# Sparse attention on TensorE: four groups of transpositions a head become two

## The chip, the core and the metric

The kernel runs on one core of one Trainium2 chip. The metric is the device time of one execution in microseconds (us), in the median of several. A core has TensorE (PE in the rows; its weight loads are listed apart as PEld), VectorE (DVE), ScalarE (ACT), GpSimd (POOL) and SyncE (SP), each with a queue of its own that it works through in order. They wait for each other through semaphores.

## The reference, cut to what matters

Two transformer blocks over 512 tokens of width 1024. The change lies in the second one's sparse attention, 16 heads of width 128. Each query attends to those 128 earlier keys that score highest with an indexer, and keys and values are shared by all heads:

```python
def dsa_mixer(x, cos_h, sin_h, cos_i, sin_i, w_in, w_out):
    topk = min(TOPK_MAX, L // 4)
    h = x @ w_in
    q = apply_partial_rope(h[..., :o1].reshape(B, L, DSA_HEADS, DSA_HEAD_DIM), cos_h, sin_h)
    k = apply_partial_rope(h[..., o1:o2], cos_h, sin_h)
    v, z = h[..., o2:o3], h[..., o3:o4]
    ...
        _, idx = lax.top_k(score, topk)             # per query, from the indexer
        k_sel, v_sel = gather(k, idx), gather(v, idx)
        logits = jnp.einsum('bthd,btjd->bthj', q_b, k_sel).astype(jnp.float32) * ATTN_SCALE
        logits = jnp.where(valid[:, :, None, :], logits, -jnp.inf)
        probs = jax.nn.softmax(logits, axis=-1).astype(v.dtype)
        return jnp.einsum('bthj,btjd->bthd', probs, v_sel)
    ...
    return (o * jax.nn.silu(z)) @ w_out
```

## The kernel before

Everything is written out by hand: the order in each engine's queue is the order of the code, and each step waits for named steps of the other engines (`S[...]`, one semaphore for each engine and stage; the tables `DSA_PE`, `DSA_ACT`, `DSA_DVE` list the names in that order). Matrix products are made of three products in a rounded format, high x high, high x low and low x high parts (`split_mm`, lines 933 to 935). A weight unit of 128x1024 comes by DMA, GpSimd splits it into its parts, and one unit is 8 blocks of 3 products with 512 columns.

The 512 queries are four tiles of 128. Tile q looks at the first q+1 tiles of keys, so its scores are 128 x 128(q+1), and the keys that the indexer didn't choose are masked out. For head n and tile q the steps are

- `s{q}` (`dsa_score`, TensorE): the scores, into bank 3 (q even) or bank 4 (q odd). Tiles 2 and 3 wait until VectorE has masked tiles 0 and 1 of the same head, since they use the same banks.
- `m{q}` (`dsa_mask`, VectorE, line 3666): scale, add the mask, and the maximum of each row through an accumulator that is read out behind it.
- `e{q}` (`dsa_exp`, ScalarE, line 2624), `r{q}` (reciprocal of the row sum, VectorE, line 3671), `n{q}` (`dsa_normalise`, ScalarE, line 2629).
- `t{q}` (`dsa_turn`, TensorE, line 1827): q+1 transpositions of 128x128 in full fp32, tile 0 into bank 5, tile 1 into bank 6, tile 2 into bank 2, tile 3 into bank 5 again (so it waits for `l0`).
- `h{q}` (ScalarE, line 1925) and `l{q}` (VectorE, line 2685): the high and the low part of the transposed tile, out of the bank.
- `o` (`dsa_values`, TensorE): 12 products with the values, once `l2`, the last of the low parts, is there.

The loop over s in TensorE's part makes one slot a head. It is filled up with the projection of the query of head s+3 (in the last heads with blocks of the output projection), block by block through `fill(first, end)`, so that TensorE has work while VectorE and ScalarE do the softmax of the tiles. In slot s stand score 1 of head s+1, tile 2 of head s, block 0, score 3, block 1, the values of head s, block 2, tile 0 of head s+1, block 3, score 2, blocks 4 and 5, tile 1, blocks 6 and 7, tile 3, and score 0 of head s+2. Slot s = -1, that of head 0, has no tile 2 and no values, and the last gate (24 products) ahead of tile 3.

Of the kernel before, what the change touches and what calls it, by code (L numbers as in the profile page):

```python
# [134 lines left out]
def dsa_unit(name):  # L135
    return U0["dsa"] + DSA_UNITS.index(name)


DSA_PE = [("s1", 1), ("t2", 0), ("s3", 1), ("o", 0), ("t0", 1), ("s2", 1), ("t1", 1), ("t3", 1), ("s0", 2)]
DSA_ACT = [("qf", 1), ("h3", -1), ("h2", -1), ("e0", 0), ("e1", 0), ("n0", 0), ("e3", 0), ("n1", 0), ("h0", 0), ("oh", -1),  # L140
           ("n3", 0), ("qh", 1), ("e2", 0), ("h1", 0), ("n2", 0), ("z", 0)]
DSA_DVE = [("l0", 1), ("ql", 2), ("r2", 1), ("ol", 0), ("l1", 1), ("m0", 2), ("m1", 2), ("l3", 1), ("l2", 1), ("sw", 3), ("r0", 2),
           ("m3", 2), ("ss", 3), ("oz", 1), ("qc", 3), ("r3", 2), ("qa", 3), ("m2", 2)]

# [4 lines left out]
def dsa_late(s):  # L149
    return [n for n in DSA_LATE if n // 2 == DH // 4 + s]  # L150


def dsa_slot(table, s):

    return [f"{op}_{s + off}" for op, off in table
            if 0 <= s + off < DH and not (op in ("oh", "ol") and s + off in DSA_LATE)]
# [55 lines left out]
def build(nc, ins, out):  # L212
    ctx = ExitStack()
    with ctx:
# [332 lines left out]
        def ln_stage(name):  # L547
            e = [f"e{m}" for m in ln_tiles(name)]
            stage(name, 1, ["ph0", "ph1", "s2n"] + [f"sq{m}" for m in range(5)] + ["sq5", e[0], "sq6", "sq7", *e[1:4], "sqrt", *e[4:-2], "hi0", e[-2], "hi1", e[-1],
                                                                            "h0", "h1"]  # L550
                  + [f"{a}{m}" for m in range(2, KD) for a in ("hi", "h")],
                  ["pl0", "pl1", "y0", "y1", "s1", "y2", "s2", "c0", "c1", "y3", "s3", "v1", "c2", "y4", "s4", "v2", "c3", "y5", "s5", "v3", "c4",
                   "y6", "s6", "v4", "c5", "y7", "s7", "v5", "c6", "c7", "v6", "mu", "dl", "dd", "v7", "var", "rs", "a0", "a1", "b0", "b1"]
                  + [x for m in M8 for x in [f"lo{m}"] + ([f"a{m + 2}", f"b{m + 2}"] if m < KD - 2 else [])],
                  ["y0", "y2", "row", "part", "y4", "y6", *projected(e[:2]), "total", *projected(e[2:4]), "squares", "mean", "root", *projected(e[4:])])
# [30 lines left out]
        for n in range(DH + 1):  # L586
            dsa_act += [f"z_{DH - 1}" if x == "z_0" else x for x in dsa_slot(DSA_ACT, n)
                        if x not in ("qf_0", "qf_1") and (x[:2] != "z_" or n == 0)]
            dsa_act += [f"oh_{x}" for x in dsa_late(n - DH + 2)]
        stage("dsa", 1, dsa_act,  # L590
              sum([dsa_slot(DSA_DVE, n) + [f"ol_{x}" for x in dsa_late(n - DH + 3)] for n in range(-3, DH)], []),
              sum([dsa_slot(DSA_PE, n) for n in range(-2, DH)], []))
        ln_stage("ln2")
# [336 lines left out]
        def _(pe):  # L930
# [70 lines left out]
            a, d, z = enter(pe, "pe", "start")  # L1001
# [7 lines left out]
            a, d, z = enter(pe, "pe", "lat", ())  # L1009
# [30 lines left out]
            a, d, z = enter(pe, "pe", "attn", ())  # L1040
# [160 lines left out]
            a, d, z = enter(pe, "pe", "mix", ())  # L1201
# [30 lines left out]
            a, d, z = enter(pe, "pe", "wo", ())  # L1232
# [28 lines left out]
            a, d, z = enter(pe, "pe", "res1", ())  # L1261
# [15 lines left out]
            for c in range(4):  # L1277
                s = (u + c) % 2
# [32 lines left out]
            for half in (0, 1):  # L1311
                name = f"up{half}"
                a, d, z = enter(pe, "pe", name, ())
# [25 lines left out]
                a, d, z = enter(pe, "pe", name, ())  # L1339
                if half == 0:  # L1340
                    with pe.Fori(0, 2) as i:
                        for m2 in range(2):
# [3 lines left out]
                            for v in range(3):  # L1346
                                c = 3 * m2 + v
                                pe.wait_ge(split_ready, i * 6 + (U0[name] + c + 1))
                                for kb in range(8):
# [6 lines left out]
                                    s = (U0[name] + c) % 2  # L1356
# [45 lines left out]
            a, d, z = enter(pe, "pe", "res2", ())  # L1402
# [24 lines left out]
            a, d, z = enter(pe, "pe", "res3", ())  # L1427
# [26 lines left out]
            a, d, z = enter(pe, "pe", "gla_a", ())  # L1454
# [12 lines left out]
            k, s = KD - 1, (u + 5) % 2  # L1467
# [20 lines left out]
            a, d, z = enter(pe, "pe", "gla", ())  # L1488
# [243 lines left out]
            a, d, z = enter(pe, "pe", "idx", ())  # L1732
# [56 lines left out]
            a, d, z = enter(pe, "pe", "dsa", ())  # L1789
# [11 lines left out]
            def dsa_gate(n):  # L1801
                if n - 2 < IDX_GATES:
                    pe.wait_ge(idx_a.sem, idx_a.at(f"z{n - 2}"))
                else:
                    pe.wait_ge(a.sem, a.at(f"z_{n - 2}"))
                unit(dsa_unit(f"z{n}"), dsa_unit(f"z{n}") % 2, 7 if n % 2 else 2, x2_hi, x2_lo)
# [12 lines left out]
            def dsa_turn(q, n):  # L1819
                pe.wait_ge(a.sem, a.at(f"n{q}_{n}"))  # L1820
                if q == 3:
                    pe.wait_ge(d.sem, d.at(f"l0_{n}"))
                elif n:
                    pe.wait_ge(d.sem, d.at(f"l{(3, 1, 2)[q]}_{n - 1}"))
                p = dsa_probs(q)
                for kt in range(q + 1):
                    mm = pe.transpose(ps[DSA_TURNED[q]][:, kt * P:(kt + 1) * P], p[:, kt * P:(kt + 1) * P], ident)  # L1827
                z.done(mm, f"t{q}_{n}")
# [41 lines left out]
            for s in range(-2, DH):  # L1870
                def fill(first, end):
                    if s >= DH - 3:
                        dsa_out(*((0, 0), (0, 1), (1, 0))[s + 3 - DH], first, end)
                    elif s >= -1:
                        dsa_projection(s + 3, first, end)

                score = 0 <= s + 1 < DH
                if score:
                    dsa_score(1, s + 1)
                if s >= 0:  # L1880
                    dsa_turn(2, s)
                fill(0, 1)
                if score:
                    dsa_score(3, s + 1)
                if s == DH - 1:
                    fill(1, 8)
                else:
                    fill(1, 2)
                if s >= 0:
                    dsa_values(s)  # L1890
                if score:
                    fill(2, 3)
                    dsa_turn(0, s + 1)
                    fill(3, 4)
                    dsa_score(2, s + 1)
                    fill(4, 6)
                    dsa_turn(1, s + 1)
                    fill(6, 8)
                    if s == -1:
                        dsa_gate(DH - 1)  # L1900
                    dsa_turn(3, s + 1)
                if s + 2 < DH:
                    dsa_score(0, s + 2)
            enter(pe, "pe", "ln2", ())
# [18 lines left out]
        def _(act):  # L1923
# [35 lines left out]
            a, d, z = enter(act, "act", "start")  # L1959
# [14 lines left out]
            a, d, z = enter(act, "act", "lat", ())  # L1974
# [34 lines left out]
            a, d, z = enter(act, "act", "attn", ())  # L2009
# [107 lines left out]
            a, d, z = enter(act, "act", "mix")  # L2117
# [10 lines left out]
            a, d, z = enter(act, "act", "wo")  # L2128
# [20 lines left out]
            a, d, z = enter(act, "act", "res1", ())  # L2149
# [32 lines left out]
            for half in (0, 1):  # L2182
                name = f"up{half}"
                a, d, z = enter(act, "act", name)
# [26 lines left out]
                a, d, z = enter(act, "act", name) if half else enter(act, "act", name, (), "up0")  # L2211
# [40 lines left out]
            a, d, z = enter(act, "act", "res2", ())  # L2252
# [18 lines left out]
            a, d, z = enter(act, "act", "ple1", ())  # L2271
# [37 lines left out]
            a, d, z = enter(act, "act", "res3", ())  # L2309
# [11 lines left out]
            a, d, z = enter(act, "act", "gla_a")  # L2321
# [20 lines left out]
            a, d, z = enter(act, "act", "gla", ())  # L2342
# [193 lines left out]
            a, d, z = enter(act, "act", "ple2", ())  # L2536
# [30 lines left out]
            a, d, z = enter(act, "act", "idx")  # L2567
# [35 lines left out]
            a, d, z = enter(act, "act", "dsa", ())  # L2603
# [27 lines left out]
            def dsa_turned_high(q, n):  # L2631
                act.wait_ge(z.sem, z.at(f"t{q}_{n}"))
                hi(a, f"h{q}_{n}", dpt_hi[:, 0:q + 1, q * P:(q + 1) * P],
                   ps[DSA_TURNED[q]][:, 0:P * (q + 1)].rearrange("p (k t) -> p k t", t=P))
# [14 lines left out]
            for s in range(DH + 1):  # L2649
                if 2 <= s + 1 < DH:  # L2650
                    dsa_query_in(s + 1)
                if s >= 1:
                    dsa_turned_high(3, s - 1)
                    dsa_turned_high(2, s - 1)
                if s < DH:
                    dsa_exp(0, s)
                    dsa_exp(1, s)
                    dsa_normalise(0, s)
                    dsa_exp(3, s)
                    dsa_normalise(1, s)  # L2660
                    dsa_turned_high(0, s)
                if s >= 1 and s - 1 not in DSA_LATE:
                    dsa_gated_high(s - 1)
                if s < DH:
                    dsa_normalise(3, s)
                    if s + 1 < DH:
                        dsa_query_high(s + 1)
                    dsa_exp(2, s)
                    dsa_turned_high(1, s)
                    dsa_normalise(2, s)  # L2670
                if s == 0:
                    dsa_silu(DH - 1)
                for n in dsa_late(s - DH + 2):
                    dsa_gated_high(n)
            layer_norm("ln2", 3, 1)
            a, d, z = enter(act, "act", "ple3", ())
# [1250 lines left out]
```

## Time and profile before

| | |
|---|---|
| time, median of 3 runs | 1691.57 us (1691.09 to 1693.63) |
| profiled execution, its own time | 1692.14 us |
| its span | 1690.4 us |
| TensorE busy | 1679.6 us, 99% of the span |
| weight loads | 1399.0 us, 83% |
| VectorE, ScalarE, GpSimd busy | 944.4, 613.8, 972.2 us |
| DMA | 152.39 MB, mean 90 GB/s |

The profile is of one execution, and times within it count from the start of its span. A page gives shares and costly groups. The trace behind it answers with a timeline (each instruction, or a run of like ones, with its start) or with the busy time of each engine in a stretch. A start is when an instruction began to run, so that the distance of two starts on TensorE is what the first of them cost; durations overlap, since the next product starts before the one before it has drained.

### The profile page before, as it was taken

To read this page: it belongs to the slowest core of one execution; us is meant where nothing else is said; L and a number is where in the kernel's file an instruction comes from. 1 tells how busy PE (TensorE), PEld (TensorE's weight loads), DVE (VectorE), ACT (ScalarE), POOL (GpSimd) and SP (SyncE) were. 2 spreads that over 40 slices of the span, in tenths; PEclk is the share of its full clock that TensorE was granted. 3 is DMA by queue.
4 is the path that set the end of the run, shared out by engine and by line. 5 is a ranking of instruction groups with operands and counts; after the bars stand their busy time and mean duration, and the time that the engine had idled before them with its cause. 6 is when DMAs were issued, how large, how long until landed. Compare 5 with 4: busy or idle time off the path is not lost.

```text
span 1690.4 us, 22071 instructions
## 1 busy us (share of the span) xinstructions
PE 1679.6 (99%) x7837; PEld 1399.0 (83%) x7837; DVE 944.4 (56%) x1633; ACT 613.8 (36%) x1167; POOL 972.2 (58%) x597
## 2 busy tenths in 40 slices
PE   9999999999999999999999999999999999999998
PEld 7888888888888888887888888888888888888887
DVE  6867422156542554166668444448667967775244
ACT  4555311243221222145633322323523137765022
POOL 6555566656666666756756565546564653333554
PEclk9999999999999999999999999999999999999999
DMA  5322222222222222333222222222232221111322
GB/s 207 90 63 80 95 98 90 99 96 92 97 100 102 99 96 101 105 100 110 94 81 81 76 94 88 75 75 94 94 97 75 99 90 54 50 54 54 92 91 80
DMA packets 57064, 152.39 MB, mean 90 GB/s; under 512 B 16912, under 2 KB 17040, under 8 KB 56976
## 3 DMA queue, kind: packets, MB, share of 16 engines
q1 hardware_dynamic: 56112, 149.63, 26.2%
q10 hardware_dynamic: 864, 1.57, 0.3%
q8 instruction: 57, 0.93, 0.2%
q14 instruction: 31, 0.25, 0.0%
HBM read 149.08 MB, written 2.10 MB: 89 GB/s over the span
## 4 chain that ended last, share of the span: by engine, by line
PE 97%; DVE 1%; issue 1%; ACT 0%; DMA 0%; POOL 0%; SPq 0%; DVEq 0%; POOLq 0%; ACTq 0%
PE bank L933 29%; PE bank L934 28%; PE bank L935 28%; PE bank L1827 1%; PE bank L1667 1%; PE bank L1670 1%; PE bank L1666 1%; PE bank L1393 1%; PE bank L1394 1%; PE bank L1397 1%; PE bank L971 1%; PE bank L1122 1%; PE bank L957 1%; PE bank L1287 0%; PE bank L1286 0%
## 5 line engine op out<-in xcount | busy, mean ns | idle before, releaser
L843 POOL TENSOR_TENSOR w_lo<-raw,w_hi 128x1024 fp32r<-128x1024 f32 (+2 forms) x275 | 643.9, 2341 | 23.0
L841 POOL TENSOR_SCALAR w_hi<-raw 128x1024 fp32r<-128x1024 f32 (+2 forms) x275 | 286.1, 1040 | 637.0 <-issue 485.4
L933 PE MATMUL bank<-op_hi,w_hi 128*128 128x512 f32 x964 | 380.5, 395 | 0.6 <-PE bank L935 0.3
L935 PE MATMUL bank<-op_hi,w_lo 128*128 128x512 f32 x964 | 375.8, 390 | 0.0
L934 PE MATMUL bank<-op_lo,w_hi 128*128 128x512 f32 x964 | 375.5, 390 | 0.0
L933 PE MATMUL bank<-r,w_hi 128*128 128x512 f32 x856 | 339.3, 396 | 0.6 <-POOL w_lo L843 0.5
L935 PE MATMUL bank<-r,w_lo 128*128 128x512 f32 x856 | 333.9, 390 | 0.0
L934 PE MATMUL bank<-r,w_hi 128*128 128x512 f32 x856 | 333.6, 390 | 0.0
L935 PEld LDWEIGHTS bank<-op_hi,w_lo 128*128 128x128 f32 x964 | 181.0, 188 | 38.3
L933 PEld LDWEIGHTS bank<-op_hi,w_hi 128*128 128x128 f32 x964 | 181.4, 188 | 37.6 <-issue 1.2
L934 PEld LDWEIGHTS bank<-op_lo,w_hi 128*128 128x128 f32 x964 | 181.4, 188 | 35.1 <-issue 0.2
L1925 ACT ACTIVATE r<-bank 128x512 fp32r<-128x512 f32 (+4 forms) x197 | 95.1, 505 | 268.6 <-DVE bank L2688 84.9
L935 PEld LDWEIGHTS bank<-r,w_lo 128*128 128x128 f32 x856 | 160.7, 188 | 34.2
L933 PEld LDWEIGHTS bank<-r,w_hi 128*128 128x128 f32 x856 | 160.9, 188 | 33.5 <-issue 1.2
L934 PEld LDWEIGHTS bank<-r,w_hi 128*128 128x128 f32 x856 | 161.0, 188 | 29.9
L2685 DVE TENSOR_TENSOR r<-bank,r 128x384 fp32r<-128x384 f32 (+5 forms) x196 | 107.8, 572 | 102.0 <-ACT r L1925 100.8
L2694 DVE SCALAR_TENSOR_TENSOR fx<-bank,gain,fx 128x511 f32<-128x511 f32 x88 | 66.0, 749 | 46.8 <-ACT fx L2192 43.0
L2688 DVE TENSOR_TENSOR bank<-bank,fx 128x512 f32<-128x512 f32 x86 | 59.8, 696 | 53.8 <-PE bank L935 48.1
L2691 DVE TENSOR_TENSOR eb<-eb,bank 128x512 f32<-128x512 f32 x48 | 32.6, 684 | 97.2 <-PE bank L935 97.0
L2688 DVE TENSOR_TENSOR fx<-bank,fx 128x512 f32<-128x512 f32 x41 | 27.8, 686 | 84.8 <-PE bank L935 84.5
L935 PE MATMUL bank<-r 128*128 128x512 f32 (+2 forms) x224 | 72.2, 323 | 0.0
L934 PE MATMUL bank<-r 128*128 128x512 f32 (+2 forms) x224 | 72.1, 322 | 0.0
(335 smaller groups left out, 2318.7 us busy)
## 6 DMA issues: line engine op xcount, KB each, us to landing
raw<-in_weights SPq DMA_DIRECT2D x267, 512.0 KB, 3.2
out<-h SPq DMA_DIRECT2D x8, 256.0 KB, 2.0
h<-in_x SPq DMA_DIRECT2D x3, 512.0 KB, 7.5
raw<-in_weights SPq DMA_DIRECT2D x8, 128.0 KB, 2.6
raw<-in_weights SPq DMA_DIRECT2D x6, 160.0 KB, 2.5
cst<-in_consts SPq DMA_DIRECT2D x1, 832.0 KB, 10.4
raw<-in_weights SPq DMA_DIRECT2D x3, 256.0 KB, 3.1
rope_cos<-in_p ACTq DMA_DIRECT2D x3, 256.0 KB, 3.8
```

The costliest lines, as they stand in the source:

```text
L841: pool.tensor_scalar(hi, raw[:, r, at:w], 1.0, 0.0, ALU.mult, ALU.add).then_inc(hi_ready, 1)
L843: pool.tensor_tensor(lo, raw[:, r, at:w], hi.bitcast(F32), ALU.subtract).then_inc(split_ready, 1)
L933: pe.matmul(o, ah, bh, start=start, stop=False, skip_group_check=skip)
L934: pe.matmul(o, ah, bl, start=False, stop=False, skip_group_check=skip)
L935: return pe.matmul(o, al, bh, start=False, stop=stop, skip_group_check=skip)
L957: mm = pe.matmul(ps[bank][:, column + t:column + t + 1], x[:, t * P:(t + 1) * P], ones[:, 0:1], start=n == 0, stop=n == len(tiles) - 1)
L971: mm = pe.matmul(out[:, t * P:(t + 1) * P], column[:, t:t + 1].to_broadcast([P, P]), ident, start=True, stop=True)
L1925: steps.done(act.activation(o, i_, ACT.Copy), name)
L2685: steps.done(dve.tensor_tensor(o, src, high.bitcast(F32), ALU.subtract), name)
L2688: steps.done(dve.tensor_tensor(o, x, y, ALU.mult), name)
L2691: steps.done(dve.tensor_tensor(o, x, y, ALU.add), name)
L2694: steps.done(dve.scalar_tensor_tensor(out=o, in0=x, scalar=s, in1=y, op0=op0, op1=op1), name)
```

## The change

Tile 1 is transposed right behind tile 0 of its head, no longer between blocks 5 and 6. Tile 2 is transposed right behind tile 3, before score 0 and score 1 of the next heads, no longer behind score 1. ScalarE copies out tile 1 right behind tile 0. The tables of names follow.

```diff
-DSA_PE = [("s1", 1), ("t2", 0), ("s3", 1), ("o", 0), ("t0", 1), ("s2", 1), ("t1", 1), ("t3", 1), ("s0", 2)]
-DSA_ACT = [("qf", 1), ("h3", -1), ("h2", -1), ("e0", 0), ("e1", 0), ("n0", 0), ("e3", 0), ("n1", 0), ("h0", 0), ("oh", -1),
-           ("n3", 0), ("qh", 1), ("e2", 0), ("h1", 0), ("n2", 0), ("z", 0)]
+DSA_PE = [("s1", 1), ("s3", 1), ("o", 0), ("t0", 1), ("t1", 1), ("s2", 1), ("t3", 1), ("t2", 1), ("s0", 2)]
+DSA_ACT = [("qf", 1), ("h3", -1), ("h2", -1), ("e0", 0), ("e1", 0), ("n0", 0), ("e3", 0), ("n1", 0), ("h0", 0), ("h1", 0), ("oh", -1),
+           ("n3", 0), ("qh", 1), ("e2", 0), ("n2", 0), ("z", 0)]
...
                 if score:
                     dsa_score(1, s + 1)
-                if s >= 0:
-                    dsa_turn(2, s)
                 fill(0, 1)
                 if score:
                     dsa_score(3, s + 1)
...
                 if score:
                     fill(2, 3)
                     dsa_turn(0, s + 1)
+                    dsa_turn(1, s + 1)
                     fill(3, 4)
                     dsa_score(2, s + 1)
-                    fill(4, 6)
-                    dsa_turn(1, s + 1)
-                    fill(6, 8)
+                    fill(4, 8)
                     if s == -1:
                         dsa_gate(DH - 1)
                     dsa_turn(3, s + 1)
+                    dsa_turn(2, s + 1)
                 if s + 2 < DH:
                     dsa_score(0, s + 2)
...
                     dsa_exp(3, s)
                     dsa_normalise(1, s)
                     dsa_turned_high(0, s)
+                    dsa_turned_high(1, s)
                 if s >= 1 and s - 1 not in DSA_LATE:
                     dsa_gated_high(s - 1)
...
                     dsa_exp(2, s)
-                    dsa_turned_high(1, s)
                     dsa_normalise(2, s)
```

TensorE's queue where one head's slot ends and the next begins, before. Line 1827 is a transposition, bank 3 takes score 0, bank 4 scores 1 and 3, bank 5 tile 3, bank 2 tile 2, and bank 1 a block of the projection:

```order
5349 L1827 MATMUL bank5<-cst,fx 128x128 x4
5350 L933 MATMUL bank3<-r2 128x128
5351 L934 MATMUL bank3<-r2 128x128
5352 L935 MATMUL bank3<-r2 128x128
5353 L933 MATMUL bank4<-r2 128x256
5354 L934 MATMUL bank4<-r2 128x256
5355 L935 MATMUL bank4<-r2 128x256
5356 L1827 MATMUL bank2<-cst,fx 128x128 x3
5357 L933 MATMUL bank1<-r2,w_hi 128x512
5358 L934 MATMUL bank1<-r2,w_hi 128x512
5359 L935 MATMUL bank1<-r2,w_lo 128x512
5360 L933 MATMUL bank4<-r2 128x512
```

The same place in the changed program:

```order
5349 L1827 MATMUL bank5<-cst,fx 128x128 x4
5350 L1827 MATMUL bank2<-cst,fx 128x128 x3
5351 L933 MATMUL bank3<-r2 128x128
5352 L934 MATMUL bank3<-r2 128x128
5353 L935 MATMUL bank3<-r2 128x128
5354 L933 MATMUL bank4<-r2 128x256
5355 L934 MATMUL bank4<-r2 128x256
5356 L935 MATMUL bank4<-r2 128x256
5357 L933 MATMUL bank1<-r2,w_hi 128x512
5358 L934 MATMUL bank1<-r2,w_hi 128x512
5359 L935 MATMUL bank1<-r2,w_lo 128x512
5360 L933 MATMUL bank4<-r2 128x512
```

Between score 1 (bank 4, 256 columns) and score 3 (bank 4, 512 columns) only one block of three products is left.

ScalarE's queue in one head, before. Bank 5 with 128x128 is the high part of tile 0, bank 6 that of tile 1; line 2629 normalises, line 2624 is the exponential:

```order
726 L2629 ACTIVATE fx<-fx,st 128x256
727 L1925 ACTIVATE r2<-bank5 128x128
728 L1925 ACTIVATE op_hi<-bank7 128x512
729 L2629 ACTIVATE fx<-fx,st 128x512
730 L1925 ACTIVATE r2<-fx 128x512
731 L2624 ACTIVATE fx,st<-fx,st 128x384
732 L1925 ACTIVATE r2<-bank6 128x2x128
733 L2629 ACTIVATE fx<-fx,st 128x384
```

And in the changed program, whose line numbers are 2 lower there:

```order
726 L2627 ACTIVATE fx<-fx,st 128x256
727 L1923 ACTIVATE r2<-bank5 128x128
728 L1923 ACTIVATE r2<-bank6 128x2x128
729 L1923 ACTIVATE op_hi<-bank7 128x512
730 L2627 ACTIVATE fx<-fx,st 128x512
731 L1923 ACTIVATE r2<-fx 128x512
732 L2622 ACTIVATE fx,st<-fx,st 128x384
733 L2627 ACTIVATE fx<-fx,st 128x384
```

Tile 1's copy-out moved ahead of four instructions, the last of them tile 2's exponential. The queues of VectorE, GpSimd and SyncE hold the same instructions in the same order.

## Rows read from the trace of the kernel before

**Rows 1.** The page, part 4: shares of the chain that ended last, by engine.
```profile
PE 97%; DVE 1%; issue 1%; ACT 0%; DMA 0%; POOL 0%; SPq 0%; DVEq 0%; POOLq 0%; ACTq 0%
```

**Rows 2.** Busy time of each engine, sparse attention: stretch, its length, busy us, clock, DMA.
```profile
1375.00:1550.00 175.00, 174.93 (x957) 149.34 (x956) 124.84 (x357) 123.75 (x304) 62.14 (x36) 1.00 0.16 55
```

**Rows 3.** Timeline, TensorE at transpositions: start us, duration us, engine, line, operation, tiles.
```profile
1416.26 0.27 PE L1827 MATMUL bank<-cst,fx 128*128 128x128 f32 x1
...
1416.60 0.39 PE L934 MATMUL bank<-r,w_hi 128*128 128x512 f32 x1
...
1546.28 0.93 PE L1827 MATMUL bank<-cst,fx 128*128 128x128 f32 x7
...
1547.27 0.39 PE L934 MATMUL bank<-op_lo,w_hi 128*128 128x512 f32 x1
```

**Rows 4.** Timeline, a steady head, from score 1 to score 3.
```profile
1421.60 0.28 PE L935 MATMUL bank<-r 128*128 128x256 f32 x1
...
1422.07 0.42 DVE L3666 CUSTOM_DVE_ANT_0 fx<-bank,fx 128x256 f32<-128x256 f32 x1
...
1422.42 0.08 DVE L3666 DVE_READ_ACCUMULATOR2_ANT st<- 128x1 f32 x1
...
1422.51 0.40 PE L935 MATMUL bank<-r,w_lo 128*128 128x512 f32 x1
1422.62 0.19 PEld L933 LDWEIGHTS bank<-r 128*128 128x128 f32 x1
...
1422.75 0.39 PE L933 MATMUL bank<-r 128*128 128x512 f32 x1
```

**Rows 5.** Timeline, head 0, from score 1 to score 3; in brackets idle before, releaser.
```profile
1376.14 0.28 PE L935 MATMUL bank<-r 128*128 128x256 f32 x1
...
1376.61 0.42 DVE L3666 CUSTOM_DVE_ANT_0 fx<-bank,fx 128x256 f32<-128x256 f32 x1
1376.73 0.39 PE L935 MATMUL bank<-r,w_lo 128*128 128x512 f32 x1
1376.96 0.08 DVE L3666 DVE_READ_ACCUMULATOR2_ANT st<- 128x1 f32 x1
...
1377.16 0.19 PEld L933 LDWEIGHTS bank<-r 128*128 128x128 f32 x1 [0.48 <-DVE st L3666]
1377.19 0.47 PE L933 MATMUL bank<-r 128*128 128x512 f32 x1
...
1377.50 0.40 PE L934 MATMUL bank<-r 128*128 128x512 f32 x1
```

**Rows 6.** Timeline, a steady head: subtractions of tiles 3 and 2, load of the values.
```profile
1422.42 1.15 DVE L2685 TENSOR_TENSOR r<-bank,r 128x512 fp32r<-128x512 f32 x2
...
1423.91 0.19 PEld L933 LDWEIGHTS bank<-r 128*128 128x128 f32 x1
```

**Rows 7.** Timeline, a steady head: tile 1 normalised, tile 0 transposed.
```profile
1425.63 0.49 ACT L2629 ACTIVATE fx<-fx,st 128x256 f32<-128x256 f32 x1
...
1426.73 0.27 PE L1827 MATMUL bank<-cst,fx 128*128 128x128 f32 x1
```

**Rows 8.** Timeline, head 0: tile 0 transposed, tile 1 normalised.
```profile
1379.36 0.33 PE L1827 MATMUL bank<-cst,fx 128*128 128x128 f32 x1
...
1380.32 0.49 ACT L2629 ACTIVATE fx<-fx,st 128x256 f32<-128x256 f32 x1
```

**Rows 9.** Timeline, head 1: tile 1 normalised, tile 0 transposed.
```profile
1395.32 0.50 ACT L2629 ACTIVATE fx<-fx,st 128x256 f32<-128x256 f32 x1
1395.35 0.27 PE L1827 MATMUL bank<-cst,fx 128*128 128x128 f32 x1
```

**Rows 10.** Timeline, a steady head: tile 1 copied out, tile 2 normalised, tile 3 transposed.
```profile
1419.40 0.39 ACT L1925 ACTIVATE r<-bank 128x256 fp32r<-128x256 f32 x1
...
1419.68 0.61 ACT L2629 ACTIVATE fx<-fx,st 128x384 f32<-128x384 f32 x1
...
1420.60 0.60 PE L1827 MATMUL bank<-cst,fx 128*128 128x128 f32 x4
```

## The prediction

> **What bounds the kernel now.** I read four views. The shares of the chain that ended last come first: 97% of the span is TensorE, so a change pays or costs only where TensorE's own row of work gets shorter or longer [rows 1]. The second is the table by stretches. It shows that in the sparse attention, 1375 to 1550 us, TensorE is busy 174.93 of 175.00 us at a granted clock of 1.00, VectorE and ScalarE about 125 us each [rows 2]. There is next to no wait left for a change of order to take away. It can still bring one in, so the question is which waits are held off only by the work that now stands between two instructions.
>
> The third view is the timeline of TensorE, for what a transposition costs. The fourth is the same timeline with VectorE, ScalarE and the weight loads beside it, at each place that the change shortens. The starts of successive products are used, not their durations, because products overlap.
>
> **What a transposition costs, and what grouping gives.** Wide products (512 columns) follow each other every 0.23 us. Tile 0's single transposition starts at 1416.26, and the second wide product behind it at 1416.60. That is 0.34 us, less one wide product of 0.23, so 0.11 for one. At the last head seven already stand in a row: from 1546.28 to the second wide product at 1547.27 are 0.99 us, less 0.23 makes 0.76, or 0.11 for each of the seven [rows 3]. The price goes by the piece, with no fixed price of a group. A head has 1+2+3+4 = 10 transpositions before and after. Two groups in place of four save nothing that I can read: I take 0. The bound on the side of a gain is that the whole 0.11 us of the single transposition is a price of its group: two groups fewer in 16 heads would give back 32 x 0.11 = 3.5 us. On the other side the group of seven shows none above the piece, so 0.
>
> **What is moved off its place: tile 2's three transpositions.** Before, they stand between head n+1's score 1 and the first block of the projection. Score 3 cannot be loaded until VectorE has masked score 1 (both use bank 4), and that takes a chain of fixed length. In the steady heads score 1's last product starts at 1421.60, the mask starts at 1422.07, its accumulator is read out by 1422.50 (1422.42 + 0.08), and score 3's weights are loaded at 1422.62, 1.02 us behind score 1's last product [rows 4]. The product follows at 1422.75. The product before it started at 1422.51, at which time the load would have run if nothing had held it. So the mask is already 0.11 us late for the load and just on time for the product. This place has no slack, and what fills it is three transpositions (0.33 us) and three wide products.
>
> After the change the three transpositions are gone from there. One head in the present trace already runs so, head 0, which has no head before it to transpose: score 1, three wide products, score 3. Score 1's last product starts at 1376.14, the mask at 1376.61, read out by 1377.04, and the load of score 3 is held to 1377.16 with 0.48 us idle before it, put down to VectorE's read-out. The products start at 1376.73, 1377.19 and 1377.50. Undisturbed that is two steps of 0.23, and it took 0.77, so TensorE lost 0.31 us [rows 5]. The load came 1.02 us behind score 1's last product, as in the steady head. From the steady side: 1422.75 less 0.33 is a start 0.82 us behind score 1, and the load is only free at 1.02. Both agree.
>
> The Trainium skill, "TensorE: Matmul & The Clock Gate", section "Step-by-step: what each phase is for", says that TensorE's queue pulls weight loads ahead of products in flight. Score 3's weights are the query, which is ready long before. If only the product had to wait for bank 4, it could start at 1377.16 instead of 1376.96, a loss of 0.20 a head. The row of head 0 speaks against it: the load itself stood idle for 0.48 us.
>
> Heads 1 to 15 lose the cover, so 15 x 0.31 = 4.65 us. Bounds: 0 if something that I don't see makes the mask earlier, and 0.33 (the whole cover) a head, 4.95. I take 0.31, since head 0 is the same sequence of instructions.
>
> Does the stall pay for something else? TensorE has no other wait in this stage to swallow it. It does help VectorE. Its two masks start 0.33 us later, because scores 0 and 1 now stand behind tile 2's transpositions, and so does the pair of subtractions of tiles 3 and 2, which ran 1422.42 to 1423.57. Done at 1423.90, it is in time for the values' load, which goes from 1423.91 to 1424.22 with the stall [rows 6].
>
> **Tile 1, moved up behind tile 0.** Its two transpositions need ScalarE's normalised tile 1. In a steady head that runs 1425.63 to 1426.12, and tile 0's transposition starts at 1426.73: ready 0.6 us early, with the stall 0.9 [rows 7]. No cost there. In head 0 there are no values of an earlier head between score 3 and tile 0, and tile 0's transposition stands at 1379.36 while tile 1 is normalised only from 1380.32 to 1380.81 [rows 8]. Due 0.11 behind tile 0, at 1379.47, it can start at about 1380.9: 1.4 us, once. Bounds 1.3 and 1.5. In head 1 ScalarE is late again, with tile 1 normalised from 1395.32 to 1395.82, and tile 0's transposition at 1395.35 [rows 9]. Tile 1 is due at 1395.46, with the stall of score 3 at 1395.77, and can start at about 1395.9 to 1396.0: 0.2 us, between 0 and 0.3. Behind the waiting transposition all of TensorE's order is queued, and nothing hides it. Score 2 comes 0.22 us later than before, and so does its mask.
>
> **Tile 2, moved ahead of scores 0 and 1.** It needs tile 2 normalised. Before, that ran 1419.68 to 1420.29, with the copy-out of tile 1 (0.39) at 1419.40 ahead of it. ScalarE now does this copy-out in front of four others, the last of them tile 2's exponential. The delay reaches at most the copy's whole 0.39 us, since it leaves its old place at the same time: ready by 1420.68 at the latest. Tile 3's four transpositions start at 1420.60 and tile 2 is due at 1420.60 + 4 x 0.11 = 1421.04, its load some 0.11 earlier [rows 10]. A slack of about 0.25 us is left: cost 0, upper bound 0.2 a head. Head 0 has a whole gate (24 wide products) in front of this place.
>
> No DMA, no GpSimd and no VectorE instruction changes its place in its queue.
>
> **Sum.** 4.65 (score 3) + 1.4 (head 0) + 0.2 (head 1) + 0 (grouping, tile 2) = 6.25, say 6.2 us. The profiled execution took 1692.14 us (its span of 1690.4 and 1.7 around it), and would take 1698.3. The median of the runs, 1691.57, stands 0.57 lower, so I predict 1697.8.
>
> **Rivals.**
> - Only the product of score 3 waits, not its load: 15 x 0.20 + 1.6 = 4.6 us, 1696.2. It needs head 0's idle load to be a special case. 3%.
> - Tile 2's wait for its normalised tile bites as well. ScalarE's delay is somewhat larger than I bound it, and 0.2 us a head is added: 6.2 + 3.0, 1700.8. The slack of 0.25 us speaks against it. 7%.
> - Score 3's wait doesn't come back in the steady heads. Head 0 might be special since ScalarE changes its table there, though the mask is VectorE's and started 0.47 us behind score 1's last product in both. Then only heads 0 and 1 pay: +1.6, 1693.2. 7%.
> - Faster: the price of 0.11 us belongs to the group, not to the piece. Two groups fewer in 16 heads give 3.5 us back, less the 1.6 of heads 0 and 1, if the mask of score 1 comes in time: 1691.57 - 3.5 + 1.6 = 1689.7. It decides the sign once score 3 loses less than 1.9 / 15 = 0.13 us a head. Against it stand the 0.76 us of the group of seven, seven times the price of the group of one, and the held load of head 0. 3%.
>
> **How the numbers follow.** The forecast as summed has 80%. Slower by over 0.2% (3.4 us, about what a measurement of this kernel tells from no change) is the forecast, the first and the second rival: 80 + 3 + 7 = 90%. Within 0.2% is the third, 7%; faster the fourth, 3%. The range runs from 1695.0, with score 3 at 0.12 a head ((1695.0 - 1691.57 - 1.6) / 15), which takes in the first rival, to 1700.8, the second.
>
> **What would show it.** In the list of waits a new row should stand, a TensorE load at line 933 released by VectorE's read-out of its accumulator, about 15 times 0.4 to 0.5 us of idle load, and 0.31 us between the products each time. A head should repeat every 10.78 us in place of 10.47 (1426.73 less 1416.26 [rows 3, 7]). In head 0 one transposition should wait about 1.4 us for ScalarE. The seven transpositions in a row should cost 0.76 us in every head. I am wrong if heads still repeat in 10.47 us, or in more than 10.9, which would be a second wait.

## The result, and the profile after

The changed kernel takes 1697.24 us (median of 8 runs, 1696.92 to 1697.67), before 1691.88 (8 runs, 1690.68 to 1693.63): 5.4 us slower. The ratio is 1.0032, with a 95% interval from 1.0024 to 1.0041. The forecast was 1697.8 us, 6.2 us more.

From the page of the changed kernel's profile, the span and the busy times:

```profile
span 1695.1 us, 22071 instructions
...
PE 1682.4 (99%) x7837; PEld 1398.3 (82%) x7837; DVE 944.0 (56%) x1633; ACT 615.7 (36%) x1167; POOL 972.3 (57%) x597
```

TensorE is still at 99%. The stretch of [rows 2] shows what is new, in the same columns:

```profile
1375.00:1550.00 175.00, 172.63 (x925) 144.46 (x925) 121.52 (x351) 122.89 (x299) 58.37 (x34) 1.00 0.16 54
```

TensorE is busy 172.63 of 175 us there, in place of 174.93. The list of waits of the weight loads (PEld) names who ended them: total, times, longest, in us.

```profile
PEld bank L933 <- DVE st L3664: 7.6, 16, 0.5
...
PEld bank L1827 <- ACT fx L2627: 2.0, 3, 1.4
```

Before, each of the two was a single short wait in head 0: that of [rows 5], and 0.3 us of tile 0. Now the first stands for the load of score 3, released by VectorE's read-out of its accumulator, in all 16 heads, and the second for three waits of transpositions. The list gives the idle time of the load, 0.47 us each. What TensorE loses has to be read from its products, in a steady head of the timeline, from score 1 to score 3 (it answers to [rows 4]):

```profile
1423.19 0.28 PE L935 MATMUL bank<-r 128*128 128x256 f32 x1
...
1423.66 0.42 DVE L3664 CUSTOM_DVE_ANT_0 fx<-bank,fx 128x256 f32<-128x256 f32 x1
1423.78 0.39 PE L935 MATMUL bank<-r,w_lo 128*128 128x512 f32 x1
...
1424.01 0.08 DVE L3664 DVE_READ_ACCUMULATOR2_ANT st<- 128x1 f32 x1
...
1424.21 0.19 PEld L933 LDWEIGHTS bank<-r 128*128 128x128 f32 x1 [0.47 <-DVE st L3664]
1424.24 0.47 PE L933 MATMUL bank<-r 128*128 128x512 f32 x1
...
1424.55 0.39 PE L934 MATMUL bank<-r 128*128 128x512 f32 x1
```

Score 1's last product starts at 1423.19, and the load of score 3 at 1424.21, 1.02 us behind, as in [rows 4] and [rows 5]. This length hasn't changed. But now only three products lie in it, the last of them starting at 1423.78, and from there to the second product of score 3 are 0.77 us in place of 2 x 0.23: 0.31 us lost.

Head 0, tile 0 and tile 1 ([rows 8]):

```profile
1378.17 0.33 PE L1827 MATMUL bank<-cst,fx 128*128 128x128 f32 x1
...
1379.13 0.49 ACT L2627 ACTIVATE fx<-fx,st 128x256 f32<-128x256 f32 x1
...
1379.68 0.20 PEld L1827 LDWEIGHTS bank<-cst,fx 128*128 128x128 f32 x2 [1.37 <-ACT fx L2627]
1379.68 0.44 PE L1827 MATMUL bank<-cst,fx 128*128 128x128 f32 x2 [1.18 <-ACT fx L2627]
```

Tile 1's load waits for ScalarE's normalised tile 1 (1379.13 to 1379.62) and begins 1.51 us behind tile 0's transposition, where 0.11 would do: 1.4 us. Head 1 ([rows 9]), where tile 0 and tile 1 are merged in one row:

```profile
1395.50 0.49 ACT L2627 ACTIVATE fx<-fx,st 128x256 f32<-128x256 f32 x1
...
1395.82 0.67 PE L1827 MATMUL bank<-cst,fx 128*128 128x128 f32 x3
...
1396.04 0.20 PEld L1827 LDWEIGHTS bank<-cst,fx 128*128 128x128 f32 x2 [0.32 <-ACT fx L2627]
```

Here tile 1's load begins 0.22 us behind tile 0's product.

To keep the stage apart from the rest, I take one length in all kernels: from the last product of head 0's score 1 to the start of the last group of seven transpositions. Before it runs from 1376.14 [rows 5] to 1546.28 [rows 3], 170.14 us. In the changed kernel it runs from 1374.95 to 1551.05, 176.10: 5.96 us more. The profiled executions differ by less, 1697.02 against 1692.14, since the changed kernel's profile enters the stage 1.19 us earlier. That comes from the first 12 us, which the change doesn't touch: 1.09 us of it stand there already (11.60 less 10.51 in the rows below). TensorE before:

```profile
6.34 2.05 PE L978 MATMUL bank<-op_hi,w_hi 128*128 128x512 f32 x4 [1.17 <-ACT op_hi L1963]
...
9.89 1.91 PE L984 MATMUL bank<-op_hi,w_lo 128*128 128x512 f32 x4
11.60 0.56 PE L933 MATMUL bank<-op_hi,w_hi 128*128 128x512 f32 x1
```

and in the changed kernel:

```profile
5.97 2.05 PE L978 MATMUL bank<-op_hi,w_hi 128*128 128x512 f32 x4 [0.81 <-ACT op_hi L1961]
...
9.53 1.15 PE L984 MATMUL bank<-op_hi,w_lo 128*128 128x512 f32 x4
10.51 0.39 PE L933 MATMUL bank<-op_hi,w_hi 128*128 128x512 f32 x1
```

The products of the first line wait for ScalarE 0.36 us less. In the group at 9.89 the next start is 1.71 us on, 0.43 a product, and in the one at 9.53 it is 0.98 us on, 0.25 a product, with the products behind it at 0.23. I read the 0.43 as the lower of the clock's two levels (1.2 GHz) and the 0.23 as the upper (2.4 GHz), since the one is nearly twice the other. The spacing alone says so: the table by stretches gives a granted clock of 1.00 in both profiles already from 5 us on. Where the length begins differs among the profiles of the nine other kernels too, the changed one and e1 to e8 (1374.73 to 1375.59), and a median over several runs depends less on it than a single profile does. So below both are given: the times, and the length of the stage.

### The profile page after: what moved, and what is told of

Read it like the earlier page. It is cut to its first block, busy times and chain, and to the rows that moved or that the text cites. A ratio compares the mean times of both kernels' runs of the same rounds, so it can differ in the third digit from the quotient of the medians.

```text
span 1695.1 us, 22071 instructions
## 1 busy us (share of the span) xinstructions
PE 1682.4 (99%) x7837; PEld 1398.3 (82%) x7837; DVE 944.0 (56%) x1633; ACT 615.7 (36%) x1167; POOL 972.3 (57%) x597
## 4 chain that ended last, share of the span: by engine, by line
PE 97%; DVE 1%; issue 1%; ACT 0%; POOL 0%; DMA 0%; SPq 0%; DVEq 0%; POOLq 0%; ACTq 0%
PE bank L933 29%; PE bank L935 28%; PE bank L934 28%; PE bank L1827 1%; PE bank L1670 1%; PE bank L1666 1%; PE bank L1667 1%; PE bank L1393 1%; PE bank L1397 1%; PE bank L1394 1%; PE bank L971 1%; PE bank L1122 1%; PE bank L957 1%; PE bank L1290 0%; PE bank L1286 0%
```

## The experiments

All were timed in five rounds against the kernel before, whose median was 1691.92 us beside e1 to e4 and 1691.75 beside e5 to e8. "Stage" is the length just defined, minus before's 170.14. "A head" is the mean distance of tile 0's transpositions from head 2 to head 15, (their starts' difference) / 13.

| kernel | time | ratio (95%) | stage | a head |
|---|---|---|---|---|
| before | 1691.9 | | 0 | 10.47 |
| the change | 1697.24 | 1.0032 (1.0024 to 1.0041) | +5.96 | 10.77 |
| e1: tile 1 alone | 1694.59 | 1.0015 (1.0006 to 1.0024) | +2.15 | 10.50 |
| e2: tile 2 alone | 1696.41 | 1.0027 (1.0017 to 1.0037) | +4.83 | 10.79 |
| e3: score 1 in bank 6 | 1693.22 | 1.0009 (1.0000 to 1.0018) | +1.59 | 10.45 |
| e4: no block between scores 1 and 3 | 1707.06 | 1.0089 (1.0074 to 1.0105) | +15.85 | 11.43 |
| e5: two blocks between them | 1692.59 | 1.0006 (0.9996 to 1.0015) | +1.45 | 10.44 |
| e6: head 0's tile 1 as before | 1696.29 | 1.0025 (1.0015 to 1.0035) | +4.85 | 10.78 |
| e7: e3, heads 0 and 1 as before | 1691.31 | 0.9997 (0.9988 to 1.0006) | -0.26 | 10.45 |
| e8: e5, heads 0 and 1 as before | 1691.40 | 0.9998 (0.9989 to 1.0007) | -0.39 | 10.44 |

**e1, tile 1 alone.** Against the changed kernel, tile 2 goes back:

```diff
                 if score:
                     dsa_score(1, s + 1)
+                if s >= 0:
+                    dsa_turn(2, s)
                 fill(0, 1)
...
                     dsa_turn(3, s + 1)
-                    dsa_turn(2, s + 1)
```

> Only tile 1 is moved up behind tile 0 (with its copy-out on ScalarE); tile 2 stays between score 1 and block 0. Theory: score 3 keeps its cover and a steady head repeats in 10.45 to 10.47 us. Head 0 waits 1.4 us for ScalarE's normalised tile 1. Head 1 waits 0.45 us, more than in the changed kernel, since score 3's stall no longer delays tile 0. Sum +1.5 to +1.9 us against before. Rival (a transposition's 0.11 us is a price of its group): one group fewer in 16 heads gives 1.8 us back, so +0.1 us and 10.36 us a head.

The stage is 2.15 us longer, the time 2.67 (interval 1.0 to 4.1). Of score 3's waits three are left in the list, 0.5 us in head 0 and 0.3 us for two others, short enough to hide behind a product. Head 1 shows what score 3's stall had been covering:

```profile
1395.28 0.49 ACT L2628 ACTIVATE fx<-fx,st 128x256 f32<-128x256 f32 x1
1395.31 0.27 PE L1827 MATMUL bank<-cst,fx 128*128 128x128 f32 x1
...
1395.83 0.20 PEld L1827 LDWEIGHTS bank<-cst,fx 128*128 128x128 f32 x2 [0.60 <-ACT fx L2628]
```

Tile 1's load now begins 0.52 us behind tile 0's product, in place of 0.22, and its idle time is 0.60. From tile 0 of head 0 to that of head 2 it takes 28.30 us, before 26.42: 1.88 for heads 0 and 1, as expected. The rest was missed. I expected 10.45 to 10.47 a head and it is 10.50, a few hundredths more from head 4 on, although a group is gone. I find no wait of TensorE behind it: some wide products follow at 0.23 where they did at 0.227. What decides between these two I can't tell. A gain of 0.11 us for a group would have made 10.36, and is ruled out.

**e2, tile 2 alone.** Against the kernel before:

```diff
                 if score:
                     dsa_score(1, s + 1)
-                if s >= 0:
-                    dsa_turn(2, s)
                 fill(0, 1)
...
                     dsa_turn(3, s + 1)
+                    dsa_turn(2, s + 1)
```

> Only tile 2 is moved behind tile 3; tile 1 and its copy-out stay where they were before. Theory: heads 1 to 15 lose 0.30 us each at score 3's load, a head repeats in 10.77 us, heads 0 and 1 have no new wait for ScalarE: +4.5 us against before. Rival (price of a group): +4.5 - 1.8 = +2.7 us and 10.66 us a head. Rival (both moves needed for the stall): no change.

Stage +4.83, time +4.49, 10.79 a head. The list of waits of the loads has the row of score 3, the same as in the changed kernel:

```profile
PEld bank L933 <- DVE st L3665: 7.6, 16, 0.5
```

Tile 2's move alone makes the repeated stall. The two halves add up to the change but for 1.0 us: 2.15 + 4.83 = 6.98, against 5.96. Of that 0.3 is head 1 (its wait for ScalarE overlaps score 3's stall). The rest is the hundredths a head just told of, (0.03 + 0.32 - 0.30) x 13 = 0.65.

**e3, score 1 in bank 6.** The order of work is that of the change; only where score 1 lands, and hence what scores 1 and 3 wait for, is different. (VectorE's mask reads score 1 from the new bank; that line is left out here.)

```diff
-                if q >= 2:
-                    pe.wait_ge(d.sem, d.at(f"m{q - 2}_{n}"))
+                if q == 2:
+                    pe.wait_ge(d.sem, d.at(f"m0_{n}"))
                 elif n:
-                    pe.wait_ge(d.sem, d.at(f"m{q + 2}_{n - 1}"))
+                    pe.wait_ge(d.sem, d.at({0: f"m2_{n - 1}", 1: f"l1_{n - 1}", 3: f"m3_{n - 1}"}[q]))
...
-                z.done(split_mm(ps[3 + q % 2][:, 0:w], ...
+                z.done(split_mm(ps[(3, 6, 3, 4)[q]][:, 0:w], ...
```

> The changed kernel with score 1 in bank 6 (that of the transposed tile 1) instead of bank 4, so that score 3 no longer waits for the mask of score 1; the order of work stays. Theory: score 3's stall is gone in all heads, a head repeats in 10.45 to 10.47 us. VectorE is still 0.33 us later than before, and the values' load, due at once, can find the low part of tile 2 some 0.1 us late: up to 0.1 us a head. Heads 0 and 1 pay 1.4 and 0.45 us as before for tile 1. Sum +1.5 to +3.3 us against before, +1.6 taken. Rival (the stall comes from somewhere else than bank 4, as from tile 2's wait for ScalarE or from the longer run of transpositions): stays at +5.4 us, 10.76 us a head.

Stage +1.59, forecast +1.6; 10.45 a head, forecast 10.45 to 10.47; time +1.30. A steady head, from score 1 over score 3 to the values:

```profile
1422.80 0.28 PE L935 MATMUL bank<-r 128*128 128x256 f32 x1
...
1423.27 0.42 DVE L3664 CUSTOM_DVE_ANT_0 fx<-bank,fx 128x256 f32<-128x256 f32 x1
...
1423.38 0.19 PEld L933 LDWEIGHTS bank<-r 128*128 128x128 f32 x1
...
1423.61 0.40 PE L933 MATMUL bank<-r 128*128 128x512 f32 x1
...
1423.62 0.08 DVE L3664 DVE_READ_ACCUMULATOR2_ANT st<- 128x1 f32 x1
1423.62 1.15 DVE L2683 TENSOR_TENSOR r<-bank,r 128x512 fp32r<-128x512 f32 x2
...
1424.75 0.40 PE L935 MATMUL bank<-r,w_lo 128*128 128x512 f32 x1
1424.82 0.19 PEld L933 LDWEIGHTS bank<-r 128*128 128x128 f32 x1
```

Score 3 is loaded at 1423.38 and its first product starts at 1423.61, before the mask of score 1 has been read out (1423.70). The last two rows are the next wait in line. The load of the values should begin with the product at 1424.75 and begins at 1424.82, 0.05 us behind the end of VectorE's subtractions at 1424.77. It is hidden behind that product, so costs nothing. In the changed kernel the stall itself makes room there, as the prediction had it ([rows 6]):

```profile
1424.01 1.15 DVE L2683 TENSOR_TENSOR r<-bank,r 128x512 fp32r<-128x512 f32 x2
...
1425.46 0.19 PEld L933 LDWEIGHTS bank<-r 128*128 128x128 f32 x1
```

The subtractions end at 1425.16 and the load comes at 1425.46.

**e4, no block between the scores.** Against the changed kernel:

```diff
-                fill(0, 1)
                 if score:
                     dsa_score(3, s + 1)
+                fill(0, 1)
```

> The changed kernel with score 3 directly behind score 1, block 0 behind it: the three wide products between them are gone as well. Theory: the chain from score 1 through its mask to score 3's load is of fixed length, so the stall grows by the whole 0.69 us to 1.0 us a head and a head repeats in 11.46 us: 15 x 0.69 = 10.4 us more than the changed kernel, +15.8 against before; head 0 adds nothing, since its tile 1 waits for ScalarE anyway. Rival (the stall is a fixed price of the new order): no more than 1 us beyond the changed kernel.

Stage +15.85, of which 9.89 beyond the change, 0.66 in each of 15 heads. Time +15.1.

```profile
1424.99 0.28 PE L935 MATMUL bank<-r 128*128 128x256 f32 x1
...
1425.81 0.08 DVE L3664 DVE_READ_ACCUMULATOR2_ANT st<- 128x1 f32 x1
...
1426.01 0.19 PEld L933 LDWEIGHTS bank<-r 128*128 128x128 f32 x1 [0.94 <-DVE st L3664]
...
1426.34 0.40 PE L934 MATMUL bank<-r 128*128 128x512 f32 x1
```

Again 1.02 us from score 1's last product (1424.99) to score 3's load (1426.01), with nothing but that product in between. Cover of 0.69 us is taken away, and a head grows by 0.66. I had expected the whole 0.69, 10.4 us beyond the change; the missing 0.03 us a head is of the size by which the spacing of wide products varies, and not followed up.

**e5, two blocks between the scores.** Against the changed kernel:

```diff
-                fill(0, 1)
+                fill(0, 2)
                 if score:
                     dsa_score(3, s + 1)
                 if s == DH - 1:
-                    fill(1, 8)
-                else:
-                    fill(1, 2)
+                    fill(2, 8)
```

> The changed kernel with score 3 behind block 1 instead of block 0, so six wide products stand between score 1 and score 3; the bank stays. Theory: 0.69 us of cover more than the changed kernel is over the 0.31 us that it lacked, so score 3's stall is gone and heads repeat in 10.45 to 10.47 us; the mask of score 3 comes up to 0.3 us later and has 0.5 us of slack before tile 1 is due. Left are heads 0 and 1 waiting for tile 1, 1.4 and 0.5 us: the sparse attention is 1.5 to 1.7 us longer than before, as with score 1 in bank 6. Rival (moving score 3 only hands the wait on, to the mask of score 3 and so to tile 1 or the values): 0.1 to 0.3 us a head, +3 to +6 us.

Stage +1.45, 10.44 a head. Score 3's wait is gone with the bank as it was, by 0.69 us more of work in front of it. It isn't handed on, but for one load of the values in one head, 0.2 us late. Score 3, later now, still reaches VectorE in time.

**e6, head 0's tile 1 as before.** Against the changed kernel:

```diff
                     dsa_turn(0, s + 1)
-                    dsa_turn(1, s + 1)
+                    if s >= 0:
+                        dsa_turn(1, s + 1)
                     fill(3, 4)
                     dsa_score(2, s + 1)
-                    fill(4, 8)
+                    fill(4, 6)
+                    if s == -1:
+                        dsa_turn(1, s + 1)
+                    fill(6, 8)
```

> The changed kernel, but in head 0 alone tile 1 is transposed between blocks 5 and 6, as before the change. Theory: the wait of 1.4 us for ScalarE's normalised tile 1 goes and nothing takes its place, since a gate of 24 products stands ahead of tile 3: sparse attention 1.4 us shorter than in the changed kernel, +4.6 us against before. Rival (the delay of head 0 was being used by a later wait): no gain against the changed kernel.

Stage +4.85, 1.11 less than the changed kernel, where 1.4 less was expected; time +4.54. Tile 0 of head 0 to that of head 1 takes 16.32 us in place of 17.65, 1.33 less, about the 1.4. The rest of the heads take 0.02 us more each, as in e2. Score 3's row in the list of the loads' waits is untouched:

```profile
PEld bank L934 <- DVE st L3669: 7.6, 16, 0.5
```

**e7 and e8, the waits taken out again.** e7 is e3, e8 is e5, both with tile 1 of heads 0 and 1 (its transpositions and its copy-out) where it was before the change. The edits of e3 and e5 and the tables of names are left out:

```diff
-                    dsa_turn(1, s + 1)
+                    if s >= 1:
+                        dsa_turn(1, s + 1)
                     fill(3, 4)
                     dsa_score(2, s + 1)
-                    fill(4, 8)
+                    fill(4, 6)
+                    if s < 1:
+                        dsa_turn(1, s + 1)
+                    fill(6, 8)
...
-                    dsa_turned_high(1, s)
+                    if s >= 2:
+                        dsa_turned_high(1, s)
...
                     dsa_exp(2, s)
+                    if s < 2:
+                        dsa_turned_high(1, s)
                     dsa_normalise(2, s)
```

> The changed kernel with score 1 in bank 6, and in heads 0 and 1 tile 1 where it was before (its copy-out too). Theory: every wait that the change brought in is gone, and a merged group is worth 0.02 us a head: the sparse attention 0.3 us shorter than before, which the times can't tell from no change. In head 0 score 3's own stall of 0.31 us goes too, but tile 0 then waits that much longer for ScalarE. Rival (price of a group, 0.11 us): 2 x 14 groups fewer, 3.1 us faster than before.

> As the run with score 1 in bank 6 and heads 0 and 1 as before, but with the bank unchanged and score 3 behind block 1 instead. Theory: the same 0.3 us shorter sparse attention than before, within noise. Rival (score 3's later mask holds up tile 1): 1 to 4 us slower than before.

Stage -0.26 and -0.39, 10.45 and 10.44 a head; the times, 1691.31 and 1691.40, can't be told from before (both intervals hold 1). With neither score 3 nor tile 1 waiting, two groups fewer leave a head 0.02 to 0.03 us shorter. That this is a price of the groups isn't shown: in e1, with one group fewer, a head is as much longer. No version beats the kernel before by more than the measurement can tell.

## Why the prediction was right, point by point

**Grouping: 0.** Right. In e7 a head takes 10.45 us with two groups against 10.47 with four. The rival that saw 0.11 us in each group would have shown 10.25, and fell. The 0.02 left is no more than the unexplained variation in the spacing of wide products.

**Score 3: 0.31 us x 15 = 4.65.** Right in mechanism, place and size. The chain of 1.02 us from score 1's last product to score 3's load stands unchanged in all 16 heads of the change, and with no block between (e4, 1.01 to 1.02). The wait goes when the bank is another (e3) or when there is more work in front of it (e5), with the order of the transpositions left as changed. Its size in the steady head is 0.31 us. From head to head it counts 0.30 (10.77 less 10.47), since the new order without the stall repeats in 10.45 (e3, e7). The rival in which the wait doesn't come back in the steady heads is refuted by the 16 waits in the list.

**The weight load.** The Trainium skill, "TensorE: Matmul & The Clock Gate", section "Step-by-step: what each phase is for", has loads pulled ahead of products in flight. In line with it, the load at 1422.62 in [rows 4] runs under the product that started at 1422.51. But in the changed kernel the load of score 3 was held back with its product, in 16 heads of 16, though its own operand was ready. The loss is 0.31 and not the 0.20 of that rival. The wait stands in the program ahead of both the load and the product; whether a load without a wait of its own would run ahead was not tried.

**Head 0: 1.4, head 1: 0.2.** Right. Head 0's first distance from tile 0 to tile 0 grew from 15.99 to 17.65 us, that is 1.66, of which 0.29 is score 3 of head 1, so 1.4. Head 1's grew from 10.43 to 10.94, 0.51, less 0.30 for score 3 of head 2: 0.2.

**Tile 2: 0, with 0.25 us of slack.** Right. In the changed kernel (it answers to [rows 10])

```profile
1420.97 0.62 ACT L2627 ACTIVATE fx<-fx,st 128x384 f32<-128x384 f32 x1 [0.23 <-DVE st L3669]
...
1421.62 0.92 PEld L1827 LDWEIGHTS bank<-cst,fx 128*128 128x128 f32 x7
1421.85 0.93 PE L1827 MATMUL bank<-cst,fx 128*128 128x128 f32 x7
```

tile 2 is normalised by 1421.59, the group's loads begin at 1421.62, and tile 2's own is the fifth of them, due at about 1422.06 (4 x 0.11 later). The seven transpositions run without a gap, and the rival of 0.2 us a head fell. The slack was 0.47 us, more than the 0.25 that I gave it.

**The values: 0.** Right, and e3 showed how near: without score 3's stall the load of the values is 0.07 us late and hidden.

**The sum.** 6.25 forecast, 5.96 in the length of the stage. The difference is 15 x 0.02, by which a head of the new order is shorter when nothing waits. I had put that at 0, and what makes it is open. The medians moved by 5.4, with an interval of 4.1 to 6.9 us that holds both, so the time alone couldn't tell 5.96 from 6.25.

## What to carry to other kernels

Work that stands between a producer and its consumer on the busiest engine is cover, whatever it is. Before moving it, measure the chain from the producer over the other engine to the consumer, here 1.02 us, and compare it with what is left between them, here 0.59 to the place of the load (1423.78 less 1423.19). A profile that shows no wait doesn't show slack: here the load was already late by 0.11 us, hidden behind a product. The first and the last turn of a loop are worth a look. Here head 0 already ran the sequence that the change made the rule, and gave the 0.31 us; and the last group of seven gave the price of a transposition.

## What the runs showed of the hardware beyond what was expected

- Wide products of 512 columns follow each other at 0.227 us or at 0.23 to 0.236, in stretches that change place when the order of the program changes a little. With the same instructions a head comes out 0.02 to 0.03 us longer or shorter (10.77 in the change and 10.79 with tile 2 alone; 10.50 with tile 1 alone, 10.47 before). I found no wait that goes with it, and its cause is open.
- The first 12 us of an execution vary by more than many edits are worth: the changed kernel's profile is 1.09 us ahead there, more than e7 or e8 differ from before. In the profile of the kernel before the wide products still followed each other at 0.43 us up to 11.60 (1.71 / 4), and in that of the changed kernel they had gone over to 0.23 before 10.51.
